# Five places for split weights round the norm boundaries of a two-layer flow-matching step, and a new order of ScalarE's work there

## The chip, the cores and the metric

The kernel runs on one core of a Trainium2 chip. Times are device microseconds; the metric is the time of one execution of the whole program, the median of three runs. Engines are named TensorE (PE in the rows), VectorE (DVE), ScalarE (ACT), GpSimd (POOL) and SyncE (SP), which issues nearly all DMAs.

## What is computed

One inference step of two layers, for 128 context tokens and 512 latent tokens, D = 1024, all in float32:

```python
for layer in range(2):
    hp, hs = modulate(xp, g[0], ...), modulate(xs, g[0], ...)      # rms_norm(x) * g * (1 + scale) + shift
    yp, ys = mixer(hp, hs)      # layer 0: retention and neighbourhood attention; layer 1: latent attention
    xp = xp + gate * rms_norm(yp, g[1]);  xs = xs + gate * rms_norm(ys, g[1])
    hp, hs = modulate(xp, g[2], ...), modulate(xs, g[2], ...)
    xp = xp + gate * rms_norm(square(relu(hp @ w1)) @ w2, g[3])    # 1024 -> 4096 -> 1024
    xs = xs + gate * rms_norm(square(relu(hs @ w1)) @ w2, g[3])
```

The shifts, scales and gates come from silu(c) @ w_ada, a product of two rows with a 1024 x 6144 matrix per layer. Each layer's mixer starts with an input projection and ends with an output projection.

## The kernel before

Everything is transposed: features lie on the partitions (8 tiles of 128), the T = 640 tokens along the free side, cut into two halves of 320 (s = 0, 1), the second with the context tokens at its end. Each float32 product is made of three fast ones: weight and operand are split into a high part (rounded, by ScalarE) and a low part (what is left, by VectorE or GpSimd), and TensorE adds lo x hi, hi x lo and hi x hi (L687 to L689).

**Pieces.** A piece is a 128 x 1024 float32 tile of a weight, 512 KB. SyncE loads it into a ring of STAGE = 4 places, `stage`, when the piece four before has been split (L528). ScalarE copies it to `w_hi` (`act_split`, L473), VectorE subtracts to get `w_lo` (`dve_split`, L482). w_hi and w_lo have two places each, piece n in n % 2, so piece n + 2 is split after the last unit that uses piece n (`piece_used`, `split_after`).

**Units.** A unit is one output tile of 128 features: 8 k tiles x 3 matmuls of 320 columns for one half (24), or 48 for both. PSUM is evacuated by the engine that STAGES names ("a" ScalarE, "d" VectorE), and a unit waits for the evacuation of two units ago (`free_pair`). Stages follow one another: out0 or out1 (output projection), then up and down of the MLP in four chunks of 1024 inner features (up00, down00 to up03, down03; up10 to down13 in layer 1), then in_c (layer 1's input projection) after down03. "sweeps" stages do all tiles for half 0, then all for half 1 (16 units; in_c 12), with the last two pieces kept and the other six (four) loaded and split again. The first chunk of an MLP is done by halves too (up00, down00 for half 0, up00b, down00b for half 1), so that half 1's norm can run beside half 0's matmuls.

**Norms beside the matmuls.** At a boundary two norms per half run in the background: y's (for the residual) and x's (for the next operand). ScalarE squares each tile (L1295), GpSimd adds the squares up (L2334), TensorE sums over partitions with 6 small matmuls (`sum_squares`, L699 and L702), ScalarE takes a root (L1302), VectorE its reciprocal (L1730), TensorE spreads it with 6 more (`spread_root`, L711). VectorE then makes residuals (L1740, L1742) or modulated tiles (L1754, L1757), ScalarE their high part hM_hi (L1307), GpSimd the low part hM_lo (L2338). These have fixed places in each engine's program by the number of the unit: tables RES8, MOD8 for half 0 in a sweep's units 8 to 15, RES16, MOD16 for half 1 in up00 and down00, RES6, MOD6 in in_c. In every unit ScalarE first did its norm work (`norm_beside`), then the split, then the evacuation; VectorE first norm work, then w_ada work, then the split, then h2's parts or the evacuation.

**w_ada.** VectorE accumulates the w_ada products with 512-column operations (L1827, L1824), a number per unit from `ada_plan`; eight use up a slab of 1 MB, which SyncE loads in the same queue as the pieces (L540), waiting until the slab two before is used up.

## Time and profile before

| | us |
|---|---|
| runs before, median of 3 (1934.78 to 1939.53) | 1934.99 |
| the profiled execution | 1935.91 |
| its span, first to last instruction | 1933.2 |

The profile is of one execution. TensorE is busy for 1780.1 us of the span, VectorE 1126.9, ScalarE 719.2, GpSimd 294.8. In the section of rows below, a row of the timeline tells when an instruction starts, how long it takes, its engine, its line, what it writes and reads, and in brackets the idle time of its engine before it and what ended it.

### The profile page before, as it was taken

To read this page: it belongs to the slowest core of one execution; us is meant where nothing else is said; L and a number is where in the kernel's file an instruction comes from. 1 tells how busy PE (TensorE), PEld (TensorE's weight loads), DVE (VectorE), ACT (ScalarE), POOL (GpSimd) and SP (SyncE) were. 2 spreads that over 40 slices of the span, in tenths; PEclk is the share of its full clock that TensorE was granted. 3 is DMA by queue.
4 is the path that set the end of the run, shared out by engine and by line. 5 is a ranking of instruction groups with operands and counts; after the bars stand their busy time and mean duration, and the time that the engine had idled before them with its cause. 6 is when DMAs were issued, how large, how long until landed. Compare 5 with 4: busy or idle time off the path is not lost.

```text
span 1933.2 us, 27205 instructions
## 1 busy us (share of the span) xinstructions
PE 1780.1 (92%) x10964; PEld 1560.6 (81%) x10964; DVE 1126.9 (58%) x1812; ACT 719.2 (37%) x1163; POOL 294.8 (15%) x300
## 2 busy tenths in 40 slices
PE   7799997779889999999988998999888999999997
PEld 3699872459879999999977896433787999999997
DVE  2667737763667776777455755556466773243335
ACT  1322215464434321312343564565354432131233
POOL 2300000243410000000142130333341000000012
PEclk9799998899899999999987998999999999999999
DMA  8254312102346646555331130000334552222232
GB/s 273 92 182 139 115 55 65 33 1 87 100 131 186 178 116 175 151 147 159 98 91 47 42 107 1 1 1 1 88 98 131 168 148 77 77 77 73 73 107 76
DMA packets 287406, 191.77 MB, mean 99 GB/s; under 512 B 14269, under 2 KB 261938, under 8 KB 287282
## 3 DMA queue, kind: packets, MB, share of 16 engines
q1 hardware_dynamic: 287282, 190.04, 33.5%
q8 instruction: 87, 1.43, 0.3%
q14 instruction: 37, 0.30, 0.1%
HBM read 186.47 MB, written 3.62 MB: 98 GB/s over the span
## 4 chain that ended last, share of the span: by engine, by line
PE 72%; DVE 13%; ACT 6%; issue 5%; POOL 3%; DMA 0%; SPq 0%; ACTq 0%; POOLq 0%; DVEq 0%
PE ps L687 18%; PE ps L688 18%; PE ps L689 18%; ACT w_hi L473 3%; PE ps L1206 3%; DVE w_lo L482 3%; DVE nt L1757 2%; PE ps L758 2%; PE ps L1216 1%; POOL rstd L2334 1%; DVE nt L1754 1%; DVE xT L1742 1%; PE ps L819 1%; PE ps L820 1%; PE ps L821 1%
## 5 line engine op out<-in xcount | busy, mean ns | idle before, releaser
L482 DVE TENSOR_TENSOR w_lo<-stage,w_hi 128x1024 fp32r<-128x1024 f32 (+1 forms) x250 | 306.5, 1227 | 566.1 <-ACT w_hi L473 566.0
L473 ACT ACTIVATE w_hi<-stage 128x1024 fp32r<-128x1024 f32 (+1 forms) x250 | 261.4, 1046 | 729.1 <-PE ps L689 631.9
L687 PE MATMUL ps<-h_hi,w_lo 128*128 128x320 f32 x1152 | 362.3, 315 | 23.4 <-DVE yT L2126 8.4
L687 PE MATMUL ps<-hM_hi,w_lo 128*128 128x320 f32 x1120 | 356.5, 318 | 18.6 <-DVE w_lo L482 11.0
L688 PE MATMUL ps<-h_lo,w_hi 128*128 128x320 f32 x1152 | 358.3, 311 | 0.0
L689 PE MATMUL ps<-h_hi,w_hi 128*128 128x320 f32 x1152 | 358.2, 311 | 0.0
L688 PE MATMUL ps<-hM_lo,w_hi 128*128 128x320 f32 x1120 | 351.3, 314 | 0.0
L689 PE MATMUL ps<-hM_hi,w_hi 128*128 128x320 f32 x1120 | 351.0, 313 | 0.0
L2334 POOL TENSOR_TENSOR rstd<-rstd,sq 128x320 f32<-128x320 f32 x98 | 107.0, 1093 | 973.8 <-ACT sq L1295 971.2
L687 PEld LDWEIGHTS ps<-h_hi,w_lo 128*128 128x128 f32 x1152 | 218.2, 189 | 30.7 <-DVE w_lo L482 18.9
L687 PEld LDWEIGHTS ps<-hM_hi,w_lo 128*128 128x128 f32 x1120 | 213.7, 191 | 30.0 <-DVE w_lo L482 14.2
L688 PEld LDWEIGHTS ps<-h_lo,w_hi 128*128 128x128 f32 x1152 | 218.6, 190 | 0.0
L689 PEld LDWEIGHTS ps<-h_hi,w_hi 128*128 128x128 f32 x1152 | 218.5, 190 | 0.0
L688 PEld LDWEIGHTS ps<-hM_lo,w_hi 128*128 128x128 f32 x1120 | 214.2, 191 | 0.2
L689 PEld LDWEIGHTS ps<-hM_hi,w_hi 128*128 128x128 f32 x1120 | 214.2, 191 | 0.2
L1827 DVE SCALAR_TENSOR_TENSOR acc_mlp<-slab_mlp,csil,acc_mlp 128x512 f32<-128x512 f32 x196 | 135.4, 745 | 0.0
L687 PE MATMUL ps<-hA_hi,w_lo 128*128 128x320 f32 x320 | 103.1, 322 | 9.9 <-POOL hA_lo L2338 9.9
L688 PE MATMUL ps<-hA_lo,w_hi 128*128 128x320 f32 x320 | 101.6, 317 | 0.0
L689 PE MATMUL ps<-hA_hi,w_hi 128*128 128x320 f32 x320 | 101.5, 317 | 0.0
L2224 DVE TENSOR_REDUCE w_lo<-ps 128x1 fp32r<-128x640 f32 x64 | 52.1, 814 | 66.5 <-PE ps L1118 46.0
L1668 ACT ACTIVATE pT<-ps 128x512 f32<-128x512 f32 x84 | 50.1, 597 | 76.4 <-PE ps L1206 73.7
L687 PEld LDWEIGHTS ps<-hA_hi,w_lo 128*128 128x128 f32 x320 | 62.2, 194 | 14.2 <-issue 14.2
(323 smaller groups left out, 2738.8 us busy)
## 6 DMA issues: line engine op xcount, KB each, us to landing
stage<-in_w_mlp_out SPq DMA_DIRECT2D x92, 512.0 KB, 4.2
stage<-in_w_mlp_in SPq DMA_DIRECT2D x80, 512.0 KB, 4.2
slab_mlp<-in_w_ada SPq DMA_DIRECT2D x28, 1024.0 KB, 5.3
stage<-in_w_in_ac SPq DMA_DIRECT2D x28, 512.0 KB, 3.8
slab_ac<-in_w_ada SPq DMA_DIRECT2D x12, 1024.0 KB, 5.9
ada_a<-in_w_ada SPq DMA_DIRECT2D x8, 1024.0 KB, 8.0
stage<-in_w_out_ac SPq DMA_DIRECT2D x14, 512.0 KB, 4.3
stage<-in_w_out_c SPq DMA_DIRECT2D x14, 512.0 KB, 4.2
```

The source lines that it names most:

```text
L473: nc.scalar.activation(w_hi[:, n % 2, 0:width], stage[:, n % STAGE, 0:width], ACT.Copy)\
L482: nc.vector.tensor_tensor(w_lo[:, n % 2, 0:width], stage[:, n % STAGE, 0:width], w_hi[:, n % 2, 0:width].bitcast(F32), ALU.subtract).then_ ...
L687: mm(out, lo[:, k], xh, start=j == 0, stop=False)
L688: mm(out, hi[:, k], xl, start=False, stop=False)
L689: last = mm(out, hi[:, k], xh, start=False, stop=j == k_tiles - 1)
L758: last = mm(ps[0:2, n % 2, 0:ADA_W], csil[:, k, :], slot[:, k, :], start=k == 0, stop=k == KD - 1)
L1206: mm(ps[:, 2 + n % 2, :], km[0:97, h, P * kb:P * (kb + 1)], q, start=True, stop=True).then_inc(m_s, 1)
L1668: f(pT[:, n % P_RING, :], ps[:, 2 + n % 2, :], ACT.Exp).then_inc(m_e, 1)
L1757: last = ts(part, part, coef[:, layer, which, k, g:g + 1], mod[:, layer, 8 * shift + k, g:g + 1], ALU.mult, ALU.add)
L1827: last = stt(acc, w, c, acc, ALU.mult, ALU.add)
L2224: nc.vector.tensor_reduce(peak[p % 2][:, 96 + j:97 + j], src, AX.X, ALU.max, negate=True).then_inc(a_max, 1)
L2334: sub(rstd[:, half(s)], rstd[:, half(s)], sq[:, k % 2, half(s)], ALU.add).then_inc(added[s], 1)
```

## The change

The split weights get three more places each, wx_hi and wx_lo, in the memory where w_ada's slabs and accumulators lie at other times. Only the stages in WIDE use them. Which place a piece takes, and after which unit it is split, comes from `split_plan`. The plan gives: in the entry stages (out0, down03, out1, down13) piece 2 is split after unit 0, pieces 3 and 4 after unit 1, 5 and 6 after unit 2, 7 after unit 3; tiles 3 to 7 stay for the second sweep (in_c: tiles 1 to 5), and tiles 2, 1, 0 are split after units 8, 9, 10 for units 13, 14, 15; the next stage's piece j is split after unit 11 + j, and so on five units ahead, until down00's (in_c's) last piece. There are 235 pieces for 250.

ScalarE's order in a unit becomes: roots, split, evacuation, then squares and high parts (`roots_beside`, `tiles_beside`). It evacuates down00, down00b, down10 and down10b in place of VectorE, and squares s2 for half 0. In down01 to down03 and their like VectorE's add comes before tiles and split. x's sum moves from the fourth to the sixth k tile of its unit and its spread to the fourth k tile of the next; its root is one unit later in the programs of both engines. up00b and up10b have no w_ada work, the full down stages six operations a unit for five, and the first slab waits for down00's (down10's) end. Some buffers (rope, ckn, kmas, xN) move to free the memory. The diff, cut to its core:

```diff
-          ("up00", 8, "half0", "a"), ("down00", 8, "half0", "d"), ("up00b", 8, "half1", "a"),
-          ("down00b", 8, "half1", "d"), ("up01", 8, "units", "a"),
...
+          ("up00", 8, "half0", "a"), ("down00", 8, "half0", "a"), ("up00b", 8, "half1", "a"),
+          ("down00b", 8, "half1", "a"), ("up01", 8, "units", "a"),
...
-PIECES = tuple((name, 2 * n - 2 if kind == "sweeps" else n) for name, n, kind, _ in STAGES)
+
+KEEP = 5
+SECOND = {8: (3, 4, 5, 6, 7, 2, 1, 0), 6: (3, 4, 5, 2, 1, 0)}
+PIECES = tuple((name, 2 * n - KEEP if kind == "sweeps" else n) for name, n, kind, _ in STAGES)
...
-    if u < n:
-        return u, 0
-    return (n - 2 + u - n if u < n + 2 else 2 * n - 1 - u), 1
+    return (u, 0) if u < n else (SECOND[n][u - n], 1)
...
-    return u if KIND[name] == "units" or u < n else u - 2
+    if u < n:
+        return u
+    tile = SECOND[n][u - n]
+    return tile if tile >= n - KEEP else u - KEEP
...
+def split_plan():
+
+
+    slots, before, after = [], [], []
+    free, last = {}, -1
+    for name, k in PIECES:
+        for j in range(k):
+            n = PIECE_AT[name] + j
+            wide = name in WIDE and (j >= 2 or name not in ENTRY)
+            allowed = range(2 + EXTRA * wide)
+            slot = min(allowed, key=lambda s: free.get(s, (-1, None)))
+            prior = free.get(slot, (-1, None))[1]
+            used, g = piece_used(n)
+            order = g if used == "unit" else UNIT_AT[name] - 1 + n / 1000
+            slots.append(slot)
+            before.append(prior)
+            at = -1
+            if prior is not None and piece_used(prior)[0] == "unit":
+                at = piece_used(prior)[1]
+            if name in ENTRY and j >= 2:
+                at = max(at, UNIT_AT[name] + (j - 1) // 2)
+            last = max(last, at)
+            after.append(last)
+            free[slot] = (order, n)
+    return slots, before, after
...
+EXTRA = 3
+WIDE = ("out0", "up00", "down00", "down03", "in_c", "out1", "up10", "down10", "down13")
+ENTRY = ("out0", "down03", "out1", "down13")
+SLOT, BEFORE, SPLIT_AFTER = split_plan()
+BY_HAND = tuple(range(PIECE_AT["out0"] + 2)) + (PIECE_AT["out1"], PIECE_AT["out1"] + 1)
...
-MOD16 = {10: (0,), 11: (1, 2), 12: (3,), 13: (4, 5), 14: (6,), 15: (7,)}
+MOD16 = {11: (0,), 12: (1, 2), 13: (3, 4), 14: (5,), 15: (6, 7)}
...
-    rate = {f"up{layer}0": 0, f"down{layer}0": 0, f"up{layer}0b": 1, f"down{layer}0b": 2}
+    rate = {f"up{layer}0": 0, f"down{layer}0": 0, f"up{layer}0b": 0, f"down{layer}0b": 2}
...
-        count = min(rate.get(name, 4 + (name[0] == "d")), end - n)
+        count = min(rate.get(name, 4 + 2 * (name[0] == "d")), end - n)
...
+        wx_hi, wx_lo = lay(110, ("wx_hi", [P, EXTRA, PIECE], F32R), ("wx_lo", [P, EXTRA, PIECE], F32R))
...
+        def hi_place(n):
+
+            return w_hi[:, SLOT[n], :] if SLOT[n] < 2 else wx_hi[:, SLOT[n] - 2, :]
+
+        def lo_place(n):
+
+            return w_lo[:, SLOT[n], :] if SLOT[n] < 2 else wx_lo[:, SLOT[n] - 2, :]
...
-            if n >= 2:
-                used, count = piece_used(n - 2)
+            if BEFORE[n] is not None:
+                used, count = piece_done(BEFORE[n])
                 act.wait_ge(used, count)
-            nc.scalar.activation(w_hi[:, n % 2, 0:width], stage[:, n % STAGE, 0:width], ACT.Copy)\
+            nc.scalar.activation(hi_place(n)[:, 0:width], stage[:, n % STAGE, 0:width], ACT.Copy)\
...
         def split_after(g):
 
-            return [n + 2 for n in range(PIECE_AT["end"] - 2) if piece_used(n) == (unit_done, g + 1)]
+            return [n for n in range(PIECE_AT["end"]) if SPLIT_AFTER[n] == g and n not in BY_HAND]
...
-                                if layer and o == OPS * G_MLP0:
-                                    sp.wait_ge(unit_done, UNIT_AT["up10"])
+                                if o == OPS * (G_MLP0 if layer else G_AC):
+                                    sp.wait_ge(unit_done, UNIT_AT[f"down{layer}0"] + 8)
                                 load_slab(o // (2 * SLAB_K))
...
-                        last_sums: {4: lambda: sum_squares(x_name, s)},
-                        last_sums + 1: {0: lambda: spread_root(x_name, s)}}.get(at)
+                        last_sums: {6: lambda: sum_squares(x_name, s)},
+                        last_sums + 1: {4: lambda: spread_root(x_name, s)}}.get(at)
...
@@ -1490,17 +1540,20 @@
                 else:
                     f(r32[:, v % 2, cols], single(g), ACT.Relu).then_inc(act_evac, 1)
                 act.wait_ge(act_evac, EVAC[g][0])
+                if s == 0:
+                    f(s2[:, v % 2, cols], r32[:, v % 2, cols], ACT.Square)
                 f(h2_hi[:, j, cols], r32[:, v % 2, cols], ACT.Square).then_inc(h2_hi_done, 1)
 
             def project_out(layer):
                 name, y_name, x_name = f"out{layer}", f"y{layer}a", f"in{layer}m"
                 for u in range(16):
-                    norm_beside(y_name, x_name, 0, 2 * layer, u - 8, RES8, 5, MOD8)
+                    roots_beside(y_name, x_name, 0, u - 8, 6)
                     split(name, u)
                     g, (j, s) = UNIT_AT[name] + u, unit_tile(name, u)
                     act.wait_ge(unit_done, g + 1)
                     square(y_name, s, u % 8, single(g))
                     f(yT[:, j, half(s)], single(g), ACT.Copy).then_inc(act_evac, 1)
+                    tiles_beside(x_name, 0, 2 * layer, u - 8, RES8, MOD8)
...
@@ -1516,20 +1569,32 @@
                         if early and name[0] == "u" and u == 0:
                             for k in (6, 7):
                                 operand(x_name, 0, k, hM_hi)
+                        at = u + 8 * (name[0] == "d")
+                        final = c == NCH - 1 and name[0] == "d"
                         if early:
-                            norm_beside(y_name, x_name, 1, 2 * layer, u + 8 * (name[0] == "d"), RES16, 9, MOD16)
+                            roots_beside(y_name, x_name, 1, at, 10)
+                        if final and layer == 0:
+                            roots_beside("y0m", "in1", 0, u - 8, 6)
+                        elif final and u == 8:
+                            square_root("y1m", 0, D)
                         ada_beside(layer, name, u)
-                        if c == NCH - 1 and name[0] == "d":
-                            if u:
-                                y_square(f"y{layer}m", name, u - 1)
-                            if layer == 0:
-                                norm_beside("y0m", "in1", 0, 1, u - 8, RES8, 5, MOD8)
-                            elif u == 8:
-                                square_root("y1m", 0, D)
+                        if name == f"down{layer}3" and u == 0:
+                            act.wait_ge(ada_acc, OPS * (G_ALL if layer else G_MLP0))
+                            act.wait_ge(ada_red, (G_ALL if layer else G_MLP0) // 2)
                         split(name, u)
                         if name[0] == "u":
                             up(name, u, v)
                             v += 1
+                        elif c == 0:
+                            g, (j, s) = UNIT_AT[name] + u, unit_tile(name, u)
+                            act.wait_ge(unit_done, g + 1)
+                            f(yT[:, j, half(s)], single(g), ACT.Copy).then_inc(act_evac, 1)
+                        elif final:
+                            y_square(f"y{layer}m", name, u)
+                        if early:
+                            tiles_beside(x_name, 1, 2 * layer, at, RES16, MOD16)
+                        if final and layer == 0:
+                            tiles_beside("in1", 0, 1, u - 8, RES8, MOD8)
...
                 f(cT[0:m, j, half(s)], single(g, slice(0, m)), ACT.Copy).then_inc(act_evac, 1)
+                if u < 6:
+                    tiles_beside("in1", 1, 1, u, RES6, MOD6)
...
-                    root(y[0], s)
+                    root(y_name, s)
+                if at == last:
+                    root(x_name, s)
+
+            def tiles_beside(y, x, s, at, residuals, tiles):
+
                 if at == 1 and s:
                     dve.wait_ge(h_lo_done[0], KD * (MOD_NO[x[0]] + 1))
                 for k in residuals.get(at, ()):
                     residual(*y, s, k)
-                if at == last:
-                    root(x[0], s)
                 for k in tiles.get(at, ()):
                     modulate(*x, s, k)
+
+            def norm_beside(y, x, s, at, residuals, last, tiles):
+                roots_beside(y[0], x[0], s, at, last)
+                tiles_beside(y, x, s, at, residuals, tiles)
 
             def project_out(layer):
...
+                            norm_beside(y, x, 1, u + 8 * (name[0] == "d"), RES16, 10, MOD16)
...
+                            roots_beside("y0m", "in1", 0, u - 8, 6)
+                        elif name == "down13" and u == 8:
+                            root("y1m", 0)
+                        if name[0] == "d" and c:
+                            dve.wait_ge(unit_done, g + 1)
+                            if s is None:
+                                y_, p_ = two(yT[:, j, :]), pair(g)
+                            else:
+                                y_, p_ = yT[:, j, half(s)], single(g)
+                            tt(y_, y_, p_, ALU.add).then_inc(dve_evac, 1)
+                        if c == NCH - 1 and layer == 0 and name[0] == "d":
+                            tiles_beside(("y0m", 0, G2, 1), ("in1", 1, A1, SHIFT1), 0, u - 8, RES8, MOD8)
                         elif c == NCH - 1 and name[0] == "d":
-                            if u == 8:
-                                root("y1m", 0)
                             for k in RES8.get(u - 8, ()):
                                 last_tile(k, 0, xN_first)
                         split(name, u)
-                        g, (j, s) = UNIT_AT[name] + u, unit_tile(name, u)
-                        cols = slice(0, T) if s is None else half(s)
                         if name[0] == "u":
-                            dve.wait_ge(act_evac, EVAC[g][0])
-                            link(tt(s2[:, v % 2, cols], r32[:, v % 2, cols], r32[:, v % 2, cols], ALU.mult))
+                            if s != 0:
+                                dve.wait_ge(act_evac, EVAC[g][0])
+                                link(tt(s2[:, v % 2, cols], r32[:, v % 2, cols], r32[:, v % 2, cols], ALU.mult))
                             v += 1
                             dve.wait_ge(h2_hi_done, v)
                             tt(h2_lo[:, j, cols], s2[:, (v - 1) % 2, cols], h2_hi[:, j, cols].bitcast(F32), ALU.subtract)\
                                 .then_inc(h2_lo_done, 1)
-                            continue
```

## Rows read from the trace of the kernel before

**Rows 1.** The page: its head, and busy time of each engine.
```profile
span 1933.2 us, 27205 instructions
...
PE 1780.1 (92%) x10964; PEld 1560.6 (81%) x10964; DVE 1126.9 (58%) x1812; ACT 719.2 (37%) x1163; POOL 294.8 (15%) x300
```

**Rows 2.** Waits of TensorE over the span: us in total, times, longest us.
```profile
PE ps L687 <- DVE w_lo L482: 16.9, 18, 3.5
...
PE ps L687 <- DVE yT L2126: 8.4, 6, 2.1
```

**Rows 3.** Stretches: us, busy (x) of PE, PEld, DVE, ACT, POOL, then PEclk, DMA.
```profile
473.49:515.38 41.89, 37.80 (x231) 36.22 (x230) 25.17 (x42) 21.48 (x43) 23.26 (x20) 0.89 0.35 101
...
515.38:545.72 30.34, 26.30 (x171) 24.99 (x170) 20.47 (x38) 14.42 (x27) 4.41 (x5) 0.99 0.37 104
...
545.72:585.02 39.30, 32.75 (x210) 31.78 (x211) 25.96 (x50) 13.01 (x20) 7.19 (x8) 0.96 0.46 136
...
588.54:613.18 24.64, 24.64 (x170) 24.64 (x169) 18.56 (x28) 13.00 (x21) 0.00 (x0) 1.00 0.65 193
968.14:1014.63 46.49, 37.79 (x231) 36.27 (x230) 28.40 (x50) 19.76 (x36) 20.54 (x23) 0.89 0.34 94
1014.63:1063.37 48.74, 40.93 (x211) 37.71 (x209) 29.23 (x55) 17.13 (x37) 14.00 (x15) 0.75 0.17 47
962.70:968.14 5.44, 5.44 (x44) 5.44 (x43) 0.67 (x2) 1.06 (x3) 0.00 (x0) 1.00 0.01 3
```

**Rows 4.** Timelines of ScalarE, VectorE and GpSimd in up00, a circle of 4.76 us.
```profile
528.72 0.47 ACT L1295 ACTIVATE sq<-xT 128x320 f32<-128x320 f32 x1 [2.51 <-DVE xT L1742]
529.10 1.05 ACT L473 ACTIVATE w_hi<-stage 128x1024 fp32r<-128x1024 f32 x1
530.05 0.42 ACT L1491 ACTIVATE r<-ps 128x320 f32<-128x320 f32 x1
...
533.48 0.47 ACT L1295 ACTIVATE sq<-xT 128x320 f32<-128x320 f32 x1 [2.51 <-DVE xT L1742]
...
530.17 1.23 DVE L482 TENSOR_TENSOR w_lo<-stage,w_hi 128x1024 fp32r<-128x1024 f32 x1 [1.49 <-ACT w_hi L473]
531.32 0.48 DVE L2114 TENSOR_TENSOR s<-r 128x320 f32<-128x320 f32 x1
...
532.25 0.48 DVE L1740 TENSOR_TENSOR nt<-yT,ps 128x320 f32<-128x320 f32 x1
532.76 0.68 DVE L1742 SCALAR_TENSOR_TENSOR xT<-nt,coef,xT 128x192 f32<-128x192 f32 x2
...
529.27 0.88 POOL L2334 TENSOR_TENSOR rstd<-rstd,sq 128x320 f32<-128x320 f32 x1 [3.87 <-ACT sq L1295]
```

**Rows 5.** TensorE's timeline in down00: two of its waits.
```profile
569.90 0.39 PE L687 MATMUL ps<-h_hi,w_lo 128*128 128x320 f32 x1 [1.73 <-DVE yT L2126]
...
551.40 0.42 PE L687 MATMUL ps<-h_hi,w_lo 128*128 128x320 f32 x1 [2.34 <-DVE h_lo L2117]
```

**Rows 6.** Timelines of TensorE and of GpSimd in out0's second sweep.
```profile
490.04 0.42 PE L687 MATMUL ps<-h_hi,w_lo 128*128 128x320 f32 x1 [1.12 <-DVE w_lo L482]
...
481.83 3.98 POOL L2334 TENSOR_TENSOR rstd<-rstd,sq 128x320 f32<-128x320 f32 x3 [0.93 <-ACT sq L1295]
```

**Rows 7.** Timelines of TensorE and of VectorE in in_c.
```profile
1029.35 0.63 PE L687 MATMUL ps<-hM_hi,w_lo 128*128 128x320 f32 x1 [3.50 <-DVE w_lo L482]
...
1023.56 1.31 DVE L1742 SCALAR_TENSOR_TENSOR xT<-nt,coef,xT 128x192 f32<-128x192 f32 x2
```

**Rows 8.** down01: VectorE, SyncE, ScalarE; then landing of all pieces (issues of L528).
```profile
724.22 3.40 DVE L1827 SCALAR_TENSOR_TENSOR acc_mlp<-slab_mlp,csil,acc_mlp 128x512 f32<-128x512 f32 x5
...
725.40 1.32 SPq L528 DMA_DIRECT2D stage<-in_w_mlp_out  x2
...
731.96 1.06 ACT L473 ACTIVATE w_hi<-stage 128x1024 fp32r<-128x1024 f32 x1 [9.14 <-DMA stage<-in_w_mlp_out]
...
DMA to landing us min/median/max: 3.0/4.2/9.8
```

83 lines of the change are left out of this document (36 added, 47 removed), and 4 rows, old and new, of the table STAGES.

## The prediction

> **What bounds the kernel now.** I read the page first: TensorE is busy for 92% of the span and ScalarE and VectorE for 37% and 58%, so only TensorE's losses count [rows 1]. The waits of TensorE, summed by what ended them, are small: 16.9 us for the low part of a weight tile and 8.4 us for a copy of yT are the largest that bear on the diff [rows 2]. That understates the loss, because a wait inside a norm sum is not listed and because half the clock costs time while the engine counts as busy. So the third view is the stretches against the undisturbed rate. Seven units of up00b take 24.64 us at clock 1.00: **3.52 us a unit** of 24 matmuls [rows 3]. A unit with a whole norm beside it (two sums and a spread) takes 5.44 us: **1.92 us a norm** [rows 3]. Against these prices, the 41.9 us from out0's unit 9 through up00's unit 0 should be 32.0 (8 units, 2 norms); 30.3 us for up00's other seven should be 24.6; 39.3 us for down00 should be 30.1; 46.5 us from down03's unit 9 through in_c's unit 0 should be 32.0; and 48.7 us of in_c's units 1 to 7, with one norm and some 2.5 us for cq's sum, its spread and three transposes, should be 29.1 [rows 3]. Layer 1 repeats the first three. With these the boundaries lose some 85 us together (9.9, 5.7 and 9.2 us, each twice, then 14.5 and 19.6); the rest of the kernel is at TensorE's rate or is attention, which the diff leaves alone.
>
> What ends the waits there is not one engine being full but two engines in lock step. In up00 a unit takes 4.75 us, and I add up the circle: ScalarE squares xT only when VectorE has written it (528.72), then splits the weight (529.10), VectorE makes its low part (530.17), the square of h2 (531.32), its low part, of the same size, and a new residual (532.25, 532.76), which ScalarE's next square waits for at 533.48 [rows 4]. 533.48 - 528.72 = 4.76 us. VectorE's own work in it is 1.23 + 2 x 0.48 + 0.48 + 0.68 = 3.35 us.
>
> **The change part by part, with E for the moment at which TensorE passes to the next unit.**
>
> *up00 and up10, units 1 to 7.* ScalarE now splits, evacuates, squares s2 and h2, and only then squares xT. The circle is cut: the split waits for TensorE alone. Then each engine needs its own work per unit: ScalarE 1.05 + 0.42 + 3 x 0.47 = 2.9 us at most, VectorE 3.35 less the 0.48 of s2 = 2.9 us [rows 4]. Both fit in 3.52. With five places a piece is split five units ahead, so a late low part is covered as well. Saved: 30.3 - 24.6 = 5.7 us, twice: **11.4**. If the places came without the new order, the circle would stay; the order is what pays here.
>
> *down00 and down10.* At 569.90 TensorE waits 1.73 us for VectorE's copy of yT, which stands behind two modulations and a split [rows 5]. The copy moves to ScalarE, behind the split: ready at E + 0.2 + 1.05 + 0.42 = E + 1.7, wanted at E + 3.5. The wait of 2.34 us for h2's low part at 551.40 goes too [rows 5]: ScalarE is through at E + 0.2 + 1.05 + 0.42 + 2 x 0.42 = E + 2.5, VectorE at E + 3.0, and the eighth k wants it at E + 3.1. What takes their place: the sum moves from the fourth to the sixth k and the spread to the fourth k of the next unit, and ScalarE takes the root only after the split and copy of the unit between, at E + 1.7; VectorE's reciprocal stands behind its split and is ready at E + 2.5, while TensorE asks at the fourth k, E + 4 x 0.44 = E + 1.75: 0.75 us lost. The last tiles are modulated one unit later and up00b's first unit waits some 0.9 us for them. So 30.1 + 0.75 + 0.9 = 31.7 against 39.3: 7.6, twice: **15.2**.
>
> *The sweeps out0 and out1, and up's first unit.* Kept tiles (five of eight) mean splits for units 13 to 15 only, long ahead; the waits of 1.12 us for a low part at 490.04 and its neighbours go [rows 6]. But the square of x's tiles now stands behind split and evacuation, at E + 2.2 to 2.9, and POOL adds them: three adds in a row took 3.98 us [rows 6], more than a unit. I take 1.5 us of wait at x's sum and 0.9 at its spread. Then come eight modulations (a product of 0.48 us and a scaling of like size, 7.6 us together), two splits (2.4 us) and a tail of ScalarE's copy and POOL's last two low parts (2.4 us): 12.4 us from the spread to the last low part. Of these 5.3 us pass before up's first unit starts; it ends 7.6 us after its start, 2.9 over its own work. 32.0 + 1.5 + 0.9 + 2.9 = 37.3, and 0.8 for half a clock after that wait: 38.1. Saved 41.9 - 38.1 = 3.8, and the same in layer 1: **7.6** [rows 3].
>
> *down03 and in_c's first unit.* VectorE adds the unit's yT first, then does residuals, then splits: 0.48 + 2 x 1.0 + 1.2 = 3.7 us, a lag of 0.2 us a unit that TensorE does not feel, as it needs the add of two units ago. The price is that modulation of the first tiles waits for unit 14's add instead of starting at the spread. 32.0 + 1.3 + 1.0 + 4.6 (operands) + 1.0 (clock) = 39.9: **6.6** saved.
>
> *in_c's units 1 to 7.* Three residuals a unit, one as long as 0.48 + 1.31 us, before a split of 1.2: this gave the wait of 3.50 us at 1029.35 [rows 7]. Splits of tiles 1 to 4 now fall before in_c, and none is left in units 1 to 5: units 2 and 3 go at 3.52, unit 4 waits 0.5 us for the sum. The operands of unit 6 are as late as before: eight modulations, each up to 1.6 us beside POOL's work as the residual was, some 12.5 us from the spread, of which 5.4 lie beside units 5 and 6: 7.1 us of wait. The stretch ran at 0.75 of full clock [rows 3], and this wait stays, so I leave 1.5 us for the clock. 29.1 + 0.5 + 0.2 + 7.1 + 1.5 = 38.4: 10.3 saved.
>
> *Fifteen pieces fewer* (250 to 235) free ScalarE, VectorE and the queue of 15 x (1.05 us, 1.23 us, 0.5 MB); all of it lay beside TensorE's work except where counted above. down13 and uq gain 0.8 and 0.5 us by the same reordering.
>
> *What is moved and may cost.* The additional places lie where the slabs of w_ada were, so up00b does no slab operation and down01 and down02 do six a unit for five. Five took 3.40 us [rows 8]; six are 4.1, and with split and add 6.1 us against 2 x 3.52 a whole unit: VectorE holds. The queue is tighter: SyncE's slab waits for the slab two before, and the next piece stands behind it. A piece issued at 725.40 was split at 731.96 only [rows 8]; with 1.05 and 1.23 us its low part was ready at 734.3, one microsecond before the unit that wants it, whole units being 7.05 apart. With 8/6 units a slab instead of 8/5, I find one piece in a stage 0.7 us late: **-1.5** for both stages (bounds 0 and -6). SyncE's new wait for down00's end is over before the queue reaches it: that slab stands behind a piece issued in up00b.
>
> **Sum.** 11.4 + 15.2 + 7.6 + 6.6 + 10.3 + 1.3 - 1.5 = 50.9 us. The profiled execution took 1935.9 us (its span 1933.2 and 2.7 around it), 0.9 above the median of the runs: 1935.0 - 50.9 = 1884.1, so **1884 us**. The terms I only bound are the operand waits at five boundaries (0 to 3 us each either way) and the clock.
>
> **Rivals.** (1) *POOL takes over at the boundaries.* Its add takes 0.88 us alone and 3.98 / 3 = 1.33 beside VectorE's split and residuals [rows 4, 6]. When VectorE works without pauses, POOL falls back more: 3 us at each of three sweeps, 4 us in in_c: 37 us saved, 1898 us. For it: VectorE is denser everywhere. Against: there are fewer splits to collide with. The Trainium skill (SBUF — State Buffer, section "SBUF: two separate sides") says that the port pair which VectorE and GpSimd share is an exclusive lock and that the loser fully blocks; the adds of 0.88 and 1.33 us agree. By that rule a POOL add can lose the whole of a VectorE split or residual, which would make this rival the likely one. (2) *The clock comes back too.* The stretches of the sweeps and in_c ran at 0.89 and 0.75 of full clock [rows 3], that is partly at 1.2 GHz for 2.4; if the shorter waits leave it at 2.4, in_c and the sweeps give 10 to 13 us more: 1873 us. The Trainium skill (TensorE: Matmul & The Clock Gate, "What's actually happening") ties the clock to the engine's recent activity; the falls here do follow its waits, but the operand waits remain in my count, so I give this less. (3) *The other side: the weight queue becomes the bound* in down01 and down02. Twelve slabs stand before a piece there. The slack is 1.0 us, so from a landing of 6.6 + 1.0 us on each costs TensorE its excess; to eat 50.9 us, landings must reach 6.6 + 1.0 + 4.2 = 11.8 us. The longest of all pieces was 9.8 us, the median 4.2 [rows 8]. At 12 us the time would be 1938. (4) *It does not do what it says*: another circle (the h2 low part, or ScalarE's copy behind a split whose data has not landed) keeps up and down at 4.4 us a unit; only the waits for w_lo go, 16.9 us [rows 2] and some clock with them, 18 in all: 1917 us.
>
> **How the numbers follow.** Forecast 0.62, with its own range 1875 to 1893; rival 1 0.18; rival 2 0.11; rival 3 0.03; rival 4 0.06. The range reaches down to rival 2 and up past rival 1: 1870 to 1902 leaves about 0.15 out. A measurement of this kernel tells some 0.3% (6 us) from no change. Faster 0.96 (all but rival 3 and a bit of 4), same 0.01, slower 0.03.
>
> **What the profile of after would show.** up00's and up10's units 1 to 7 at 3.52 us with no wait for w_lo; down00 near 31 us; no wait of TensorE for yT; in_c without the 3.50 us; 235 splits on each engine; down01 and down02 still at 58.1 us a stage. The count is wrong if up00 stays at 4.7 us a unit (order does not matter), if POOL's adds grow past 1.5 us each with TensorE waiting for rstd (rival 1), or if TensorE waits for w_lo in down01 (rival 3).

## The result and the profile after

The changed kernel takes **1910.6 us** (median of 4 runs, 1908.3 to 1910.8) against 1935.2 for the kernel before in the same job: a ratio of 0.9865, 95% interval 0.9848 to 0.9882. The direction was right. The gain, 24.7 us, is less than half of the 50.9 us forecast, and the time lies above the range.

The page of the changed kernel, its head and busy times (answers to [rows 1]), then TensorE's waits over the span (answers to [rows 2]):

```profile
span 1908.9 us, 27129 instructions
...
PE 1773.7 (93%) x10964; PEld 1559.0 (82%) x10964; DVE 1104.3 (58%) x1749; ACT 716.7 (38%) x1196; POOL 290.6 (15%) x300
```

```profile
PE ps L734 <- POOL hM_lo L2410: 17.5, 17, 6.0
PE ps L746 <- POOL rstd L2406: 10.6, 5, 3.6
...
PE ps L734 <- DVE w_lo L529: 1.1, 1, 1.1
```

The same view of the kernel before has these two lines, which the forecast left aside:

```profile
PE ps L687 <- POOL hM_lo L2338: 7.5, 11, 1.0
PE ps L699 <- POOL rstd L2334: 5.8, 4, 3.3
```

So the waits that the change was to remove are gone: a weight's low part 16.9 us to 1.1, yT 8.4 us to nothing [rows 2]. Two others took their place, both on GpSimd: the low part of an operand (hM_lo) rose from 7.5 to 17.5 us, the sum of squares (rstd) from 5.8 to 10.6 us. 24 us of those two went, 15 came.

The stretches of [rows 3] in the changed kernel, with the same columns (us, then busy and count of PE, PEld, DVE, ACT, POOL, then PEclk and DMA). In order: out0's unit 9 to up00's first; up00's other seven; down00; down03's unit 9 to in_c's first; in_c's units 1 to 7; then layer 1's three.

```profile
474.02:513.92 39.90, 35.04 (x231) 33.74 (x230) 27.29 (x42) 20.08 (x43) 21.67 (x20) 0.96 0.38 106
513.92:538.64 24.72, 24.72 (x171) 24.72 (x170) 19.30 (x34) 17.36 (x34) 4.07 (x5) 1.00 0.44 128
538.64:569.97 31.33, 30.53 (x212) 30.16 (x211) 15.96 (x33) 12.09 (x24) 6.74 (x8) 1.00 0.29 85
955.66:1004.78 49.12, 38.37 (x231) 37.35 (x230) 31.43 (x50) 19.08 (x35) 23.69 (x23) 0.86 0.31 84
1004.78:1047.23 42.45, 37.52 (x209) 34.08 (x209) 26.98 (x52) 14.01 (x35) 13.63 (x15) 0.80 0.06 19
1387.23:1429.82 42.59, 38.49 (x232) 37.37 (x230) 27.32 (x42) 20.59 (x43) 21.67 (x20) 0.86 0.35 99
1429.82:1455.27 25.45, 25.45 (x171) 25.45 (x170) 19.04 (x33) 16.84 (x34) 3.78 (x5) 0.97 0.44 125
1455.27:1486.60 31.33, 30.53 (x213) 30.16 (x211) 16.21 (x34) 12.10 (x24) 7.02 (x8) 1.00 0.29 85
```

The reader is to see that up00 and down00 are where they were forecast (24.72 and 31.33 us), and that one stretch got worse: from down03's unit 9 to in_c's first 49.12 us, for 46.49 before. Its two causes are rows of their own. TensorE's waits there, then what ScalarE and SyncE do ahead of the longer one, then VectorE in down03 (start us, us, engine, line, operation):

```profile
976.24 0.80 PE L746 MATMUL ps<-ones,rstd 128*128 128x1 f32 x6 [3.62 <-POOL rstd L2406]
...
996.93 0.64 PE L734 MATMUL ps<-hM_hi,w_lo 128*128 128x320 f32 x1 [6.00 <-POOL hM_lo L2410]
...
989.32 2.71 SPq L575 DMA_DIRECT2D stage<-in_w_in_c_swap  x3
...
993.84 1.06 ACT L520 ACTIVATE w_hi<-stage 128x1024 fp32r<-128x1024 f32 x1 [5.70 <-DMA stage<-in_w_in_c_swap]
...
995.17 1.17 ACT L1354 ACTIVATE hM_hi<-nt 128x320 fp32r<-128x320 f32 x3
...
967.70 0.47 DVE L2186 TENSOR_TENSOR yT<-yT,ps 128x320 f32<-128x320 f32 x1
...
968.61 1.09 DVE L1807 SCALAR_TENSOR_TENSOR xT<-nt,coef,xT 128x320 f32<-128x320 f32 x1
...
970.61 1.90 DVE L529 TENSOR_TENSOR w_lo<-stage,w_hi 128x1024 fp32r<-128x1024 f32 x1
972.43 0.47 DVE L2186 TENSOR_TENSOR yT<-yT,ps 128x320 f32<-128x320 f32 x1
```

SyncE issues the loads of in_c's pieces 4, 5 and 6 at 989.32 only, behind its wait for the end of down03 and three loads for attention. ScalarE splits piece 4 right after down03's last unit now, since there are places for it; it stands at that split for 5.70 us, and the operands that TensorE needs first (hM_hi at 995.17) stand behind it. And VectorE's round in down03 takes 972.43 - 967.70 = 4.73 us, for units of 3.52 us.

Cause one and cause two are the subject of the first experiments; the others ask what the places and the order are worth, and what the rest of the low parts' lateness is.

### The profile page after: what moved, and what is told of

Its sections match the earlier page's. It is cut to its first block, busy times and chain, and to the rows that moved or that the text cites. A ratio compares the mean times of both kernels' runs of the same rounds, so it can differ in the third digit from the quotient of the medians.

```text
span 1908.9 us, 27129 instructions
## 1 busy us (share of the span) xinstructions
PE 1773.7 (93%) x10964; PEld 1559.0 (82%) x10964; DVE 1104.3 (58%) x1749; ACT 716.7 (38%) x1196; POOL 290.6 (15%) x300
## 3 DMA queue, kind: packets, MB, share of 16 engines
q8 instruction: 88, 1.44, 0.3%
HBM read 178.87 MB, written 3.62 MB: 96 GB/s over the span
## 4 chain that ended last, share of the span: by engine, by line
PE 77%; DVE 9%; ACT 5%; issue 4%; POOL 3%; DMA 2%; SPq 0%; ACTq 0%; DVEq 0%; POOLq 0%
PE ps L734 20%; PE ps L736 19%; PE ps L735 19%; PE ps L1253 3%; PE ps L805 2%; PE ps L1263 1%; POOL rstd L2406 1%; ACT w_hi L520 1%; DMA stage<-in_w_mlp_out 1%; PE ps L866 1%; PE ps L867 1%; PE ps L868 1%; DVE nt L1822 1%; DVE w_lo L529 1%; PE ps L749 1%
## 5 line engine op out<-in xcount | busy, mean ns | idle before, releaser
L520 ACT ACTIVATE w_hi<-stage 128x1024 fp32r<-128x1024 f32 (+1 forms) x189 | 198.2, 1051 | 714.5 <-PE ps L736 560.3
L529 DVE TENSOR_TENSOR w_lo<-stage,w_hi 128x1024 fp32r<-128x1024 f32 (+1 forms) x189 | 236.8, 1256 | 379.5 <-ACT w_hi L520 379.0
L734 PE MATMUL ps<-hM_hi,w_lo 128*128 128x320 f32 x984 | 310.4, 315 | 13.2 <-POOL hM_lo L2410 12.9
L734 PE MATMUL ps<-h_hi,w_lo 128*128 128x320 f32 x872 | 271.0, 311 | 3.7 <-DVE h_lo L2199 2.6
L736 PE MATMUL ps<-h_hi,w_hi 128*128 128x320 f32 x872 | 269.4, 309 | 0.0
L735 PE MATMUL ps<-h_lo,w_hi 128*128 128x320 f32 x872 | 269.4, 309 | 0.0
L734 PEld LDWEIGHTS ps<-h_hi,w_lo 128*128 128x128 f32 x872 | 163.7, 188 | 7.9 <-DVE h_lo L2199 3.7
L735 PEld LDWEIGHTS ps<-h_lo,w_hi 128*128 128x128 f32 x872 | 163.7, 188 | 0.0
L736 PEld LDWEIGHTS ps<-h_hi,w_hi 128*128 128x128 f32 x872 | 163.7, 188 | 0.0
L734 PE MATMUL ps<-h_hi,wx_lo 128*128 128x320 f32 x280 | 88.2, 315 | 0.0
```

The costliest lines, as they stand in the source:

```text
L520: nc.scalar.activation(hi_place(n)[:, 0:width], stage[:, n % STAGE, 0:width], ACT.Copy)\
L529: nc.vector.tensor_tensor(lo_place(n)[:, 0:width], stage[:, n % STAGE, 0:width], hi_place(n)[:, 0:width].bitcast(F32), ALU.subtract).then_ ...
L734: mm(out, lo[:, k], xh, start=j == 0, stop=False)
L735: mm(out, hi[:, k], xl, start=False, stop=False)
L736: last = mm(out, hi[:, k], xh, start=False, stop=j == k_tiles - 1)
```

## The experiments

A stretch is named "down03 to in_c" if it is the fourth above, "out0 to up00" if it is the first, "out1 to up10" if it is the sixth. Times are medians of four runs (of three for e14_rate_combined); ratios are against the kernel before in the same job.

### The loads of in_c

The pieces are issued ahead of the waits and of the three loads for attention, which stay in their order:

```diff
+            for j in range(STAGE, dict(PIECES)["in_c"]):
+                load_piece("in_c", j)
             sp.wait_ge(unit_done, UNIT_AT["in_c"])
...
-            for j in range(STAGE, dict(PIECES)["in_c"]):
-                load_piece("in_c", j)
```

> One edit to the changed kernel: SyncE issues the loads of in_c's pieces 4, 5 and 6 ahead of its wait for the end of down03, not behind it and behind three other transfers. Theory (the queue that the forecast did not follow): ScalarE's split of in_c's piece 4, which the change put behind down03's last unit, no longer waits for its transfer (5.70 us in the changed kernel), so the operands behind it are written at once: the first unit of in_c falls from 16.99 us to 9 to 11, the stretch from down03's tenth unit to in_c's first from 49.1 to 42 to 44, the whole to 1902 to 1905. Rival (GpSimd's low parts are late by themselves, since VectorE's subtraction on the split runs beside them): the wait for the low part stays at 3 us or more and the whole gains under 3 us (1908 or more).

Measured: 1907.3 us, 0.9847 (0.9822 to 0.9871), 3.2 us less than the changed kernel: too little to be told by the totals, so the stretch decides. It and TensorE's waits in it (us, times, longest):

```profile
954.52:1000.81 46.29, 39.64 (x231) 38.61 (x230) 32.01 (x50) 19.33 (x35) 24.64 (x23) 0.82 0.32 89
```

```profile
PE ps L746 <- POOL rstd L2406: 3.6, 1, 3.6
PE ps L734 <- POOL hM_lo L2410: 3.0, 2, 1.9
```

The low part's 6.00 us fell to 1.9: the queue was the cause of 4 us of that wait. But in_c's first unit came to 12.9 us, not 9 to 11, the stretch to 46.3, not 42 to 44, and the whole to 1907.3, not 1902 to 1905: part of the gain stayed in a low clock (0.82 for 0.86), and 1.9 us of wait has another cause.

### The order alone, the places alone

Order alone (everything else that the change moved stays too: the square and yT's copy on ScalarE, the later sums, w_ada's rate):

```diff
-KEEP = 5
-SECOND = {8: (3, 4, 5, 6, 7, 2, 1, 0), 6: (3, 4, 5, 2, 1, 0)}
+KEEP = 2
+SECOND = {8: (6, 7, 5, 4, 3, 2, 1, 0), 6: (4, 5, 3, 2, 1, 0)}
-EXTRA = 3
+EXTRA = 0
```

> The changed kernel with two places for split weights and two tiles kept, as before the change; ScalarE's new order, the activation that makes the square, the transfer waits and the later sums stay. Theory (the order broke the circle in up00 and up10, the places did little): up00 and up10 keep their 25 us for units 1 to 7 (5.5 us less than before each); down00 and down10 keep most of their gain of 8 us; with 16 us to 22 us saved in these four stages the whole is 1913 to 1921. Rival (the places carry the change, the order alone moves the wait to the split behind it): up00 at 29 us or more, the whole 1928 to 1940.

Measured: **1907.2 us**, 0.9858 (0.9835 to 0.9882). The places take nothing off the time of the changed kernel: without them it is no slower. The stretches down00, down03 to in_c, in_c, and all of down13 (out0 to up00 has 39.92 us, up00 24.72):

```profile
538.39:569.72 31.33, 30.53 (x212) 30.16 (x211) 20.60 (x36) 15.05 (x27) 8.52 (x8) 1.00 0.47 135
954.63:999.72 45.09, 38.88 (x231) 37.33 (x230) 32.76 (x51) 19.86 (x36) 25.21 (x23) 0.86 0.36 97
999.72:1044.00 44.28, 37.38 (x209) 33.82 (x209) 28.90 (x55) 16.28 (x37) 13.94 (x15) 0.83 0.19 51
1827.75:1889.71 61.96, 59.80 (x407) 58.48 (x405) 33.80 (x47) 21.12 (x31) 14.99 (x12) 1.00 0.27 77
```

out0 to up00, up00 and down00 equal the changed kernel's to 0.02 us; in down00 VectorE and ScalarE are busier. Against it the places save 1.8 us in in_c and 2.2 us in down13 (59.72 there), and cost 4.0 us in down03 to in_c: the wait of 6.00 us by the load above is 1.77 here and the one at x's sum 0.81 for 3.62, while waits for a weight's low part, 3.6 us, come back. The profiled execution is the slowest of the four (1912.9 us), so these stretches are less sure than the median. The theory held in kind, but its range (1913 to 1921) lies above what was measured: the places are worth less here than it thought.

Places alone: in ScalarE's program, the call that squares x's tiles and writes the operands moves ahead of the split and the evacuation, in all three places where it stands:

```diff
+                    tiles_beside(x_name, 0, 2 * layer, u - 8, RES8, MOD8)
                     split(name, u)
...
-                    tiles_beside(x_name, 0, 2 * layer, u - 8, RES8, MOD8)
```

> The changed kernel with five places and five tiles kept, but ScalarE does the norm's squares and operands of a unit ahead of the split and the evacuation of that unit, as before the change. Theory: the operands are no longer behind the split that waits for its transfer, nor behind the evacuation of the last unit, so the waits for a low part at up00's first unit (2.00 us) and at in_c's first (6.00 us) shrink, while the circle in up00 and up10, and the waits of down00, come back in part (3 to 6 us in each of four stages): 1912 to 1925. Rival (the split places alone carry the gain, and the order only cost): below 1908.

Measured: 1917.8 us, 0.9908 (0.9889 to 0.9926), within the theory's numbers. up00's seven units and down00, then two of ScalarE's squares in up00:

```profile
515.55:542.43 26.88, 25.49 (x170) 24.79 (x170) 16.94 (x31) 16.18 (x33) 4.40 (x5) 0.99 0.41 116
542.43:576.29 33.86, 30.75 (x210) 30.22 (x211) 20.04 (x36) 13.32 (x26) 6.59 (x7) 1.00 0.28 80
```

```profile
523.47 0.47 ACT L1342 ACTIVATE sq<-xT 128x320 f32<-128x320 f32 x1 [1.67 <-DVE xT L1807]
...
527.75 0.47 ACT L1342 ACTIVATE sq<-xT 128x320 f32<-128x320 f32 x1 [1.67 <-DVE xT L1807]
```

ScalarE's squares are 4.28 us apart, each right behind VectorE's tile, from 523.47 into down00: the circle is still there, as the forecast said of places without the order. It is 0.48 us shorter than the 4.76 us before [rows 4], as much as the square of h2 that VectorE no longer makes. But TensorE is held by it less: up00 comes to 26.9 us, where the changed kernel has 24.7 and before 30.3 [rows 3], and its first wait in the stage is at 533.92, for an evacuation. That it is the weights split ahead that let TensorE run on is argued from there being no wait for a weight's low part in the stage. So the places, together with the square and yT's copy on ScalarE, take 3.5 of the 5.6 us, the order the rest, while the order with these two takes all of it (e2_order_alone). No run has only the two moved operations, so what they bring by themselves, here and in down00 (33.86 us for 39.30 before), is not shown; it may be a good part of what both runs have in common.

The operand waits the theory wanted to shrink are only partly smaller: out0's is 1.44 us for 2.00, and in_c's first unit has one of 3.3 us for 6.00.

### w_ada at five operations a unit

```diff
-        count = min(rate.get(name, 4 + 2 * (name[0] == "d")), end - n)
+        count = min(rate.get(name, 5), end - n)
```

> The changed kernel with w_ada's operations at five a unit in all stages from up01 on, not four in up stages and six in down01 and down02. Theory (six operations of about 0.66 us fill VectorE's unit, the sums' wait makes down units late): down01 and down02 fall from 59.3 and 59.1 us to 57.9 each, the up stages stay at their time: the whole 1907 to 1908.5. Rival (up stages, with split, square and low part on VectorE beside five operations, take the loss): up01 or up02 over 57.5 us, the whole 1910 to 1914.

Measured: 1908.5 us, 0.9858 (0.9837 to 0.9879). The totals can't tell 2 us. From up01's start to down03's, in the changed kernel and then in this one:

```profile
628.07:920.80 292.73, 291.63 (x1994) 285.13 (x1993) 209.97 (x305) 76.32 (x93) 0.00 (x0) 1.00 0.53 151
```

```profile
627.68:919.04 291.36, 291.36 (x1994) 285.13 (x1993) 210.67 (x305) 76.21 (x93) 0.00 (x0) 1.00 0.53 154
```

1.4 us less. down01 is at 57.95 us for 59.31, down02 at 58.40 for 59.13, up03 at 58.03 for 58.39, but up02 at 59.03 for 57.95: eight small matmuls of w_ada's sums, some 1.0 us, run there now and not later. The wait of 1.10 us for a weight's low part in down01 (738.20 in the changed kernel) is gone. So the theory's cause holds for down01; its size for the two stages (2 to 3.5 us with both at 57.9) was too high, and down01 takes 58.4 us in other kernels with six operations a unit (e5_tiles_first).

### Down03: residual tiles first

With the early loads, and in VectorE's program for down03:

```diff
+                        if c == NCH - 1 and layer == 0 and name[0] == "d":
+                            tiles_beside(("y0m", 0, G2, 1), ("in1", 1, A1, SHIFT1), 0, u - 8, RES8, MOD8)
                         if name[0] == "d" and c:
                             dve.wait_ge(unit_done, g + 1)
...
-                        if c == NCH - 1 and layer == 0 and name[0] == "d":
-                            tiles_beside(("y0m", 0, G2, 1), ("in1", 1, A1, SHIFT1), 0, u - 8, RES8, MOD8)
```

> The changed kernel with two edits: SyncE's early loads of in_c's pieces (as in the run e1_loads), and in down03 VectorE makes the two residual tiles of a unit ahead of its addition of that unit's sums, not behind it. Theory (the residual tiles stand behind an addition that waits for the unit's end, so x's squares end up to a unit late): the wait for the sum of squares in down03's fourteenth unit falls from 3.63 us to the 1.7 us that out0's has, that unit from 10.73 us to 7, and the whole from the 1907.3 us of e1_loads to 1902 to 1905. Rival (the additions are late instead, and TensorE waits for its banks or for the squares of y): units 10 to 12 of down03 grow from 3.52 us and the whole stays at 1906 to 1909.

Measured: **1901.1 us**, 0.9816 (0.9801 to 0.9832), 6 us less than e1_loads, in another job and with intervals that just overlap, and just under the theory's 1902 to 1905. The stretch down03 to in_c, TensorE's waits in it, and VectorE in the same units as above:

```profile
954.00:997.75 43.75, 39.54 (x232) 38.44 (x230) 28.19 (x50) 17.90 (x35) 20.65 (x23) 0.84 0.34 94
```

```profile
PE ps L734 <- POOL hM_lo L2410: 2.2, 2, 2.0
PE ps L746 <- POOL rstd L2406: 1.8, 1, 1.8
```

```profile
962.72 1.21 DVE L529 TENSOR_TENSOR w_lo<-stage,w_hi 128x1024 fp32r<-128x1024 f32 x1
963.86 0.48 DVE L1805 TENSOR_TENSOR nt<-yT,ps 128x320 f32<-128x320 f32 x1
964.37 0.66 DVE L1807 SCALAR_TENSOR_TENSOR xT<-nt,coef,xT 128x320 f32<-128x320 f32 x1
...
966.44 1.50 DVE L529 TENSOR_TENSOR w_lo<-stage,w_hi 128x1024 fp32r<-128x1024 f32 x1
967.86 0.47 DVE L1805 TENSOR_TENSOR nt<-yT,ps 128x320 f32<-128x320 f32 x1
```

The wait for the sum fell from 3.6 to 1.8 us as the theory said. The row also shows more than it said: VectorE's round is now 967.86 - 963.86 = 4.0 us for 4.73, with the same work in it, because the residual takes 0.66 for 1.09 us and the split 1.21 to 1.50 for 1.90. These operations are longer when GpSimd works beside them; that the new order moved them out of its way is argued from these rows, not tried by itself.

### Roots early, operands first, and four edits together

Roots early: ScalarE's root and VectorE's reciprocal of x's norm stand at the head of the unit that sums, not of the next.

```diff
-                    roots_beside(y_name, x_name, 0, u - 8, 6)
+                    roots_beside(y_name, x_name, 0, u - 8, 5)
```

(and 10 to 9 in up00 to down00, 6 to 5 in down03, 5 to 4 in in_c; VectorE's the same.)

> The changed kernel with ScalarE's square root and VectorE's reciprocal of x's norm one unit earlier, ahead of the split and the evacuation of the unit that sums the squares. Theory: each wait of 0.80 us for the reciprocal (out0's, down00's, down10's) goes, VectorE's modulation starts some 2 us earlier, and the first unit of up00, 10.18 us, falls by 0 to 1: the whole 1906 to 1909. Rival (the spread of the root then meets the next thing that is late, or the sum is itself late by GpSimd's additions): under 1 us gained, 1909.5 or more.

Measured: 1909.6 us, 0.9858 (0.9838 to 0.9879): no gain that can be told. Yet down00 fell from 31.33 to 30.27 us and its wait of 0.80 us is gone, twice. What was won there was lost to the clock: out0 to up00 ran at 0.89 where the changed kernel's had 0.96, and took 40.92 us for 39.90, though TensorE waited 0.8 us less in it; down03 to in_c took 50.90 us for 49.12, at 0.81 for 0.86, with the same waits.

Operands first: ScalarE writes the operands of the unit before the sweep's last (tiles 0 to 2; one where the norm lies in up00 and down00) ahead of the split, in out0 and out1 thus, and in down03 and in_c alike:

```diff
+                    operands_ahead(x_name, 0, u - 8, MOD8)
                     split(name, u)
...
                     tiles_beside(x_name, 0, 2 * layer, u - 8, RES8, MOD8)
```

> The changed kernel with ScalarE's first operands of x's norm (three of them, one where the norm lies in up00 to down00) ahead of the split and evacuation of that unit, since the unit before the last has ScalarE idle for 3 us there; all others stay. Theory (operands wait behind an evacuation that waits for TensorE, so GpSimd's low parts start 2 to 4 us late): the wait of 2.00 us for a low part in the first unit of up00 and of up10 falls under 1 us, in_c's first to third low parts come earlier too (1.49 us at its seventh unit), and with less idle time the clock stays at 2.4 GHz more often: the whole 1900 to 1906. Rival (the late low part is made late by VectorE, whose split of 1.89 us stands between the modulations, or by GpSimd slowed beside it to 1.84 us): the wait stays at 1.5 us or more, the whole 1908 to 1911.

Measured: 1907.5 us, 0.9848 (0.9832 to 0.9864), not told from the changed kernel. The wait in up00's first unit was 1.83 us for 2.00, so the rival was right: the first operands are not what is late.

All four edits on the changed kernel (early loads, residual tiles first, roots early, operands first):

> The four edits together on the changed kernel: early loads, residual tiles ahead of the additions in down03, roots a unit early, first operands ahead of the split. If each wait is a term of its own, their gains add up: 3 for the loads, 3 for the tiles, 2 for the roots, 4 to 8 for the operands, so 1893 to 1899. If they lie on one chain (GpSimd's additions and low parts), the sum falls short: 1900 to 1905.

Measured: 1899.2 us, 0.9806 (0.9787 to 0.9824): 1.9 us below e5_tiles_first, between the two ranges. The gains do not add up to what each was priced at, but e6_roots_early and e7_operands_first had shown no gain of their own to add, so this run does not settle whether one chain is the reason.

### Five tiles before the splits, with five places and with two

On e5_tiles_first:

```diff
-MOD8 = {6: (0, 1, 2), 7: (3, 4, 5)}
+MOD8 = {6: (0, 1, 2, 3, 4), 7: (5,)}
```

and ScalarE writes operands 0 to 2 ahead of the split of that unit, 3 and 4 behind its evacuation, 5 ahead of the next split.

> On e5_tiles_first: VectorE modulates tiles 0 to 4 in the unit before the sweep's last, ahead of its split, and only tile 5 in the last; ScalarE writes operands 0 to 2 ahead of that unit's split, 3 and 4 behind its evacuation, 5 ahead of the next split. Theory (the low parts are a chain on GpSimd and VectorE that starts late because both engines do first what no one waits for: splits made five units ahead): the wait of 2.01 us for a low part in up00's, in_c's and up10's first unit falls under 0.7 us, each of these units from 10.2 to 11.8 us to 6 to 8.5, the whole from 1901.1 to 1891 to 1896. Rival (GpSimd's seven low parts at 0.95 us, 1.84 beside a split, set the time by themselves, as e7_operands_first hinted): the wait stays at 1.5 us or more, the whole at 1899 to 1902.

> e5_tiles_first with two places for split weights and two tiles kept, as before the change. Theory from e2_order_alone (the places take away only short waits for a low part of a weight, about 1 us a unit in down03's units 10 to 12 and in in_c): 4 to 6 us slower than e5_tiles_first's 1901.1, so 1904 to 1908. Rival (the places do nothing once the loads are early): 1899 to 1903.

> e9_five_tiles with two places for split weights and two tiles kept. Theory (the order of e9_five_tiles borrows its time from splits that are made far ahead; with two places the next unit waits for that split): the waits for a weight's low part come back at the sweeps' last units, 1 to 3 us at each of three boundaries, so 6 to 12 us slower than e9_five_tiles. Rival (a split fits in anyway): within 4 us of it.

The two-place kernels have the edit of e2_order_alone. Measured in one job: five tiles with five places **1894.8 us**, 0.9786 (0.9769 to 0.9803); with two places 1901.1 us, 0.9817 (0.9800 to 0.9833); e5_tiles_first with two places 1906.8 us, 0.9845 (0.9828 to 0.9862). The stretch down03 to in_c with five tiles and five places (out0 to up00 has 39.5 us), and TensorE's waits around up00's first unit:

```profile
953.20:993.68 40.48, 37.12 (x231) 35.87 (x230) 28.03 (x50) 18.40 (x35) 21.60 (x23) 0.89 0.37 102
```

```profile
PE ps L747 <- POOL rstd L2416: 1.1, 1, 1.1
PE ps L735 <- POOL hM_lo L2420: 1.1, 1, 1.1
```

The low part's wait fell from 2.0 to 1.1 us, not under 0.7, and a wait for y's sum of 1.1 us appeared: GpSimd adds y's square behind the five low parts. up00's first unit takes 9.73 us, not 6 to 8.5. The whole still lands in the theory's range, so that hit is in part luck. With two places the first unit waits 0.5 us for a weight's low part (0.9 in in_c, 1.6 again in in_c's unit 4): 6.3 us in all by the medians, 6.0 by the ratios. For the pair without the five tiles, over two jobs, the ratios give 0.0029, 5.6 us. So the places are worth some 6 us once the load is in time (the theory for e10 holds, that for e11 only at its lower end and with waits of 0.5 to 0.9 us for its 1 to 3: the five tiles borrow little from them), and nothing before that.

### The combination

On e9_five_tiles: roots early, the spread of x's root at the third k, and down00's operands one unit earlier.

```diff
-                        last_sums + 1: {4: lambda: spread_root(x_name, s)}}.get(at)
+                        last_sums + 1: {2: lambda: spread_root(x_name, s)}}.get(at)
...
-MOD16 = {11: (0,), 12: (1, 2), 13: (3, 4), 14: (5,), 15: (6, 7)}
+MOD16 = {10: (0,), 11: (1, 2), 12: (3,), 13: (4, 5), 14: (6,), 15: (7,)}
```

> e9_five_tiles with the roots a unit earlier (as e6_roots_early), the spread of x's root at the third k in place of the fifth, and down00's operands one unit earlier than the change has them. Theory: the 0.80 us waits go, VectorE starts modulating 1 to 2 us earlier, and up00b's and up10b's first units lose their 1.2 us: 3 to 6 us less than e9_five_tiles, 1887 to 1892. Rival (the clock takes back what the waits give, as in e6_roots_early): under 2 us less.

Measured: **1883.4 us**, 0.9728 (0.9706 to 0.9750). up00b's eight units take 28.55 us for the changed kernel's 29.36, down00 30.27, down03 to in_c 38.05 us at clock 0.97. The gain on e9_five_tiles is 11 us where the theory had 3 to 6: the terms it named went, and the clock gave more on top. Part of that is luck. Some 2.5 us of the profiled execution's gain lie at out1's first units, which the edit does not touch, and e14_rate_combined below, with the same order at the boundaries, spends 66.80 us on down03 where this kernel spends 63.65.

### Is the low part late because of VectorE's split?

In the changed kernel, in out0 to up00, VectorE and GpSimd (start us, us):

```profile
505.49 1.89 DVE L529 TENSOR_TENSOR w_lo<-stage,w_hi 128x1024 fp32r<-128x1024 f32 x1
...
505.35 0.95 POOL L2406 TENSOR_TENSOR rstd<-rstd,sq 128x320 f32<-128x320 f32 x1
506.26 3.66 POOL L2410 TENSOR_TENSOR hM_lo<-nt,hM_hi 128x320 fp32r<-128x320 f32 x3
```

One edit, for the three pieces that are split there; the kernel leaves out most of their low part:

```diff
             dve.wait_ge(w_hi_done, n + 1)
+            if n in NARROW:
+                width = 16
...
```

> The changed kernel, with three of VectorE's 235 splits (the ones that run at the last unit of out0, down03 and out1) cut from the whole piece to 16 columns, so that most of three low parts of weights is left out. Nothing else moves. Theory (GpSimd and VectorE hinder each other: the split takes 1.89 us for 1.22 and the low part beside it 1.84 for 0.95, and both stand in the chain of low parts): GpSimd's low parts all take under 1.1 us there, the wait of 2.00 us for a low part in up00's and up10's first unit falls to 0.3 to 1.2 us. Rival (the low part is late only since its operand is, and the 1.84 us are slack): the wait stays at 1.7 us or more.

Measured: 1906.2 us, 0.9850 (0.9835 to 0.9864). GpSimd, VectorE and TensorE at the same place:

```profile
503.51 0.95 POOL L2410 TENSOR_TENSOR rstd<-rstd,sq 128x320 f32<-128x320 f32 x1
504.43 4.33 POOL L2414 TENSOR_TENSOR hM_lo<-nt,hM_hi 128x320 fp32r<-128x320 f32 x5
...
503.65 0.84 DVE L533 TENSOR_TENSOR w_lo<-stage,w_hi 128x16 fp32r<-128x16 f32 x1
...
505.34 0.42 PE L738 MATMUL ps<-hM_hi,w_lo 128*128 128x320 f32 x1 [1.02 <-POOL hM_lo L2414]
```

Five low parts take 4.33 us, 0.87 each, where three took 3.66, one of them 1.84 (the second from 508.06, the third from 508.98). The wait falls from 2.00 to 1.02 us, and up10's from 2.01 to 1.03: inside the theory's 0.3 to 1.2. In the changed kernel the addition, the split and the low part, 0.95 + 1.22 + 0.95 = 3.1 us of work, take the 2.75 us from 505.35 to 508.10: the two engines work nearly one after the other. So about half of the wait is the two engines hindering each other. That VectorE also comes sooner to its next tiles is not what did it: TensorE waits for the first of the five low parts, whose tile was modulated before the split. The other half is not shown by this run; GpSimd starts late (502.63, after 4.36 us of idle time for its first operand) and has four operations ahead of that low part. Note the 16-column operation: 0.84 us beside GpSimd's 0.95. It too sat through the addition beside it.

### The rate again, and the residual tiles

The rate by the edit of e4_rate_five, on e12_combined:

> e12_combined with w_ada's operations at five a unit everywhere from up01 on, as in e4_rate_five. Theory (the loss in down01 and down02 is a term of its own): 1.5 to 2.5 us less than e12_combined's 1883.4, down01 and down02 at 58.1 us each. Rival (the gain of e4_rate_five came from elsewhere): same within 1 us.

Measured: 1888.2 us, 0.9752 (0.9733 to 0.9772). By the medians that is 5 us more than e12_combined's 1883.4; the intervals of the ratios overlap (0.9706 to 0.9750 there). From up01 to down03 it has 291.37 us for 291.89. Of the 5.8 us between the profiled executions some 3 are in one place, down03's units 13 and 14. Unit 14, first in e12_combined, then here; the wait of 1.84 us ahead of it is the same in both:

```profile
971.39:975.58 4.19, 4.19 (x33) 4.19 (x31) 3.57 (x8) 1.94 (x4) 1.97 (x2) 1.00 0.32 84
```

```profile
973.38:979.23 5.85, 5.85 (x32) 5.85 (x31) 3.91 (x9) 1.97 (x5) 2.29 (x3) 0.69 0.32 90
```

The theory failed in its size (0.5 us for 1.5 to 2.5), and in the total the clock covered it, which fell here and not there. down01 reached the 57.95 us, down02 did not (58.40), and up02 took 59.04.

The residual tiles, on that kernel:

```diff
-RES8 = {1: (0, 1), 2: (2, 3), 3: (4, 5), 4: (6, 7)}
+RES8 = {1: (0, 1, 2), 2: (3, 4), 3: (5, 6), 4: (7,)}
```

> e14_rate_combined with the eight residual tiles of out0, down03 and out1 made 3, 2, 2 and 1 a unit, not 2, 2, 2 and 2. Theory (the last squares are late because VectorE makes their tiles late): the wait of 1.72 us for the sum of squares in the fourteenth unit falls under 1 us in each of three sweeps, 2 to 4 us less than e14_rate_combined. Rival (GpSimd adds three squares a unit, some 3 us of a 3.5 us unit, and is the limit itself): the wait stays at 1.4 us or more, no gain.

Measured: **1878.8 us** (1878.6 to 1878.9), 0.9708 (0.9694 to 0.9723), 9 us less than e14_rate_combined and the best of all. The stretches out0 to up00 and down03 to in_c (out1 to up10 has 36.4 us too):

```profile
472.42:508.82 36.40, 34.26 (x232) 33.49 (x230) 27.23 (x42) 20.81 (x43) 22.92 (x20) 0.94 0.41 117
...
948.52:984.49 35.97, 33.95 (x232) 33.11 (x230) 28.48 (x50) 18.53 (x35) 22.41 (x23) 0.97 0.41 114
```

TensorE no longer waits for x's sum of squares in any of the three sweeps. GpSimd, which the rival held to be the limit, does the same additions in time. The three waits were 1.73, 1.84 and 1.72 us in e14_rate_combined, 5.3 us together. The gain is above the theory's 2 to 4 us; the clock gave the rest, some 3 us each in down03 and out1, where TensorE had run at half clock behind these waits, less what came back at up10's first unit.

## Why the prediction was wrong

Forecast against the profiled executions (1933.2 to 1908.9 us of span, 24.3 us; forecast 50.9, so 26.6 us to explain). 19.6 us of it lie in four stretches. For each the forecast added a price of undisturbed work (32.0 us, in in_c 29.1), waits, and a term for the clock. The measured counterparts are TensorE's idle time and its busy time above that price:

| | forecast: waits + clock | measured: idle + busy above the price |
|---|---|---|
| out0 to up00 | 5.3 + 0.8 | 4.86 + 3.04 |
| out1 to up10 | 5.3 + 0.8 | 4.10 + 6.49 |
| down03 to in_c | 6.9 + 1.0 | 10.75 + 6.37 |
| in_c's units 1 to 7 | 7.8 + 1.5 | 4.93 + 8.42 |
| together | 25.3 + 4.1 | 24.6 + 24.3 |

**The step that failed is the clock term: 4.1 us in the sum, 24.3 measured.** The waits came out right as a sum, because in_c's were 2.9 us better than forecast and down03's 3.9 worse. Before the change the same four stretches had 26.2 us idle and 27.3 us busy above the price, with this row for the one that [rows 3] does not show:

```profile
1401.65:1443.13 41.48, 35.89 (x231) 34.06 (x230) 25.16 (x42) 21.49 (x43) 23.25 (x20) 0.93 0.36 102
```

So the forecast, while it held rival 2 (the clock comes back) to be unlikely, had counted some 23 us of returned clock in its own sum, for waits that by its own count were to stay about as long as they were (26.2 us before, 25.3 forecast). The waits that went were replaced by others, and the clock stayed low with them. Not all of the 24.3 us is the clock: the least that such a sweep was busy in any run is 33.95 us (e15_residuals, at 0.97), so up to 2 us in each may be a price of the norms that was set too low.

Point by point:

- **up00 and up10.** Forecast 24.6 us each, measured 24.72 and 25.45, the second at clock 0.97. Right. Its remark that the order is what pays here is borne out as far as it goes: with the order and no places the stage is the same (e2_order_alone), with the places and no order the circle stays at 4.28 us (e3_places_alone).
- **down00 and down10.** Forecast 31.7 us each with up00b's first unit; measured 31.33 us in the stage, with the 0.80 us wait for the reciprocal where 0.75 was forecast, and 1.2 us at up00b where 0.9 was counted. Some 0.8 us too good, twice. e6_roots_early took the first term back, e12_combined both.
- **The sweeps and up's first unit.** Forecast 38.1 us each, measured 39.90 and 42.59: 6.3 us short. The terms at x's sum (1.5 us; measured 1.70) and at its spread (0.9; 0.80, in out0 alone) were right. The low part's wait in up's first unit was the right kind and size (2.9 us; the waits are 2.4). The term that was mis-sized is the clock. The two stretches have nearly the same waits (4.86 and 4.10 us) and differ by 2.7 us, at clock 0.96 and 0.86.
- **down03 to in_c.** Forecast 39.9 us, measured 49.12: 9.2 us, the largest error, 5.4 of it busy time above the price and 3.9 waits. Two steps failed beside the clock. First, the sentence that prices VectorE's round at "0.48 + 2 x 1.0 + 1.2 = 3.7 us, a lag of 0.2 us a unit that TensorE does not feel": the round measured 4.73 us, since beside GpSimd's additions the split took 1.90 us and one residual in two 1.5. The lag is 1.2 us a unit, it made x's squares late, and TensorE waited 3.62 us for their sum. Second, a queue that was not followed: the split of in_c's piece 4 moved to down03's last unit, but its load stayed behind a wait for the end of that unit. The split was counted as work that moves; the data it waits for was not. e1_loads took 4 us of the wait of 6.00 and 2.8 us of the stretch away, e5_tiles_first another 2.5 us: 43.75 us, still 3.9 over the forecast, with waits of 4.2 us and a clock of 0.84. e12_combined and e15_residuals, at 38.05 and 35.97 us, show that 39.9 was to be had, but not by this change alone.
- **in_c's units 1 to 7.** Forecast 38.4, measured 42.45: 4.1 us. Units 2 to 4 went as forecast and the wait of 3.50 us [rows 7] is gone; the waits are 4.9 us for 7.8, and the clock is what was short (0.80; 1.5 us were counted).
- **w_ada.** Forecast -1.5 us, measured 290.93 us before and 292.73 after: -1.8. Right in kind and size: one late low part in down01 costs 1.10 us. Rival 3, the weight queue as the bound, did not come.
- **out1's first two units**, not in the forecast, took 13.28 us for 10.72, at clock 0.74 for 1.00, with the same wait of 3.3 us between them. The second runs at full clock in e5_tiles_first and e12_combined, so this is no effect of the change that can be shown.

The errors are 9.2, 6.3, 4.1, 2.6, 1.7, 1.0 and 0.3 us, some 25 of 26.6. Another 0.7 is uq, which gained nothing where 0.5 us was counted. The rest is not placed; the end behind down13, which the forecast left as it was, took 21.25 us for 19.45.

**The rivals.** Rival 1 (GpSimd takes over) has the nearest time, 1898 us, and its waits are the two largest rows of the profile after. But it got there by waits of 3 to 4 us more at each of four places, and these did not come: the forecast's own waits hold as a sum, and the one place that has 3.9 us more owes it to the load as well. GpSimd's additions reached 1.27 to 1.46 us in down03, not past the 1.5 that the forecast had named as its sign. That its number is near is luck. What it said of the two engines is so: one low part took 1.84 us beside the split, which took 1.89, and 0.85 when the split is cut (e13_narrow_split). The Trainium skill (SBUF — State Buffer, section "SBUF: two separate sides") says that VectorE and GpSimd lock each other out; by that rule, the trace agrees: 1.89 us for 1.22 and 1.84 for 0.95 in one place. Rival 2 (the clock comes back) did not come with the change: the mean granted clock was the same before and after, 0.956. It came in part with e12_combined (0.961). Rival 4 did not come.

**The mechanism.** The change removed what ended the waits in the profile before, and behind each stood the next chain: square, addition, sum, root, spread, modulation, operand, low part. It is this chain that sets the end of a boundary. The change put the split and evacuation ahead of ScalarE's part of it, which lengthened it by little: with ScalarE's part first (e3_places_alone) out0's waits are 0.64 and 1.44 us for 1.70 and 2.00. It left VectorE's split ahead of the modulation, which cost more (e9_five_tiles). The runs that took steps of that chain forward gained 32 us beyond the change, with the same places and nearly the same work, much of it as clock.

## What to carry to other kernels

When a step is moved earlier, follow everything that it waits for, above all the load: find the issue in the queue and the wait ahead of it, and ask what stands behind the moved step on its own engine. When two resources are removed as bounds at once (places and order here), price each alone, for each may bring most of it and their gains don't add. Price the clock by the stretch before: when the waits of a stretch are forecast to stay as long as they were, its busy time above the undisturbed price should be forecast to stay too. And work far ahead of its use belongs behind the work on the chain, not before it: places buy slack only if the order of the engines spends it.

## What the runs showed of the hardware

A 128x320 addition or low part on GpSimd takes 0.85 to 0.95 us in most places. Beside VectorE's split of 1024 columns one low part took 1.84 us, and the split 1.89 for 1.22. VectorE's residual, 128x320 with a scalar, takes 0.55 us, and 0.66 or 1.09 beside GpSimd's additions. A 16-column split took 0.84 us beside one of GpSimd's additions.

TensorE's clock after the same wait is not the same from kernel to kernel: with 1.84 us of wait ahead in both, down03's unit 14 took 4.19 us at 1.00 of 2.4 GHz in one and 5.85 us at 0.69, part of it at 1.2 GHz, in the other; out1's second unit took 3.5 us in some kernels and 5.6 in others. With the waits for x's sum gone (e15_residuals) the three sweeps ran at full clock over units 9 to 15, 28.8, 28.7 and 28.8 us at 1.00.
